# Prompt attention of a hybrid decoder layer in packs of up to eight key blocks, and merge gates stored raw

## Chip, core and metric

One Trainium2 chip, one of its cores. The metric is the device time of one execution in microseconds (us). The kernel before takes 1359.62 us, the median of 3 runs (1356.57 to 1366.08).

## What is computed

One layer of a decoder trunk, for a prompt of 1024 tokens and for 8 sequences of 4 new tokens with 512 tokens in a cache (32 more rows). The width D is 1024, all data is fp32. In short:

```python
h = rms_norm(x) * norm_g
(q, kv, gate, z_a, q_g, k_g, v_g, a_low, z_b, merge) = split(h @ w_in)
# NSA attention: 8 query heads in 2 groups of 4 (G = 2, R = 4), head width 64
o_cmp = softmax over compressed keys (one per 16 tokens)
o_slc = softmax over 16 selected blocks of 64 keys   # a prompt of 1024 has 16: all causal keys
o_win = softmax over a window of 512 keys
o_nsa = (g0 * o_cmp + g1 * o_slc + g2 * o_win) * silu(z_a)      # g0, g1, g2: sigmoid(gate)
o_g   = rms_norm(gated linear attention(q_g, k_g, v_g, a_low)) * gla_g * silu(z_b)
g_a, g_b = split(merge)
mix   = sigmoid(g_a) * (o_nsa @ w_branch_a) + sigmoid(g_b) * (o_g @ w_branch_b)
y     = rms_norm(x + mix @ w_out) * final_norm_g
```

Scores carry a bias linear in the distance (ALiBi), `-slope * distance`. The new key and value rows, the new window buffers and the states of the linear attention are outputs too.

## The kernel before

Activations and weights are split into a high and a low part (fp32r), and a projection is three products: high x high, low input x high weights, high input x low weights. The projections are done in **units**: one unit is a third of the 1056 rows for one weight tile, 8 x 3 products of 352 columns (L240), into one bank of PSUM. There are 132 units, 117 of them (NE) up to the last group of heads and 15 (NLATE) beside it. Their banks alternate, 3 and 2 (`unit_of`, L317), so that a unit needs the bank of the unit but one before it to be read (`unit_out`, L325). ScalarE takes a unit out of its bank (L360); for the kinds za, zb, ma and mb with a sigmoid (L359), for the others as a copy. For za and zb VectorE then multiplies the bank by it (L373, L375). With the last unit of a tile ScalarE rounds a coming weight tile to its high part (L219), VectorE subtracts the low part (L227). A unit leaves for HBM from one of five buffers, by a DMA of SP. Units 34 to 45 are of za, 46 to 69 of zb, 70 to 93 of ma, 94 to 116 of mb.

The **main attention** is the stage in question. A row of work n = (r, i, br) is a head r of each group, 128 queries i (0 to 7) and a branch br (0 selected, 1 window). It has i + 1 key blocks of 128 keys, at most 5 in the window: 64 rows and 264 blocks. The two groups g are computed beside each other, so each block is two score passes, two transposes and two value passes. Blocks are cut in order into steps of four: 66 steps. Per row, in this order:
- `scores` (L1633 to L1647): TensorE multiplies queries by keys, into bank g.
- `score` on VectorE (L1985 to L2004): adds the bias, writes the scores to sP in SBUF and keeps the row's extreme for the exponential.
- `probs` on ScalarE (L2236 to L2246): the exponential over a whole row, in place in sP, and its sum (128 instructions, a table load where the engine comes from a sigmoid).
- `transposes` (L1649 to L1663): TensorE turns the blocks of a step, into banks 4 and 5; ScalarE copies bank 4 to pPT (`pT_copy`, L2248, its instruction at L2199), VectorE bank 5 (L2012).
- `values` (L1665 to L1681): TensorE multiplies by the values, into a region of bank 6 or 7 for each row.
- After each four rows `spread` (L1683 to L1697): the weights `gate / sum` are formed on VectorE (`weigh`, L2018 to L2031), turned and spread over 64 rows by 16 products of `ident` by `wcol`, copied out by ScalarE (L2199), multiplied into the outputs by VectorE (`drain`, L2033 to L2038), and added to oTn by GpSimd (L1853 to L1860). There are 16 of these.

The order is written by hand in each engine's loop. On TensorE (L1793 to L1822) step m is: the units of that step, transposes(m), values(m-1), scores(m+3), and a spread where four rows have ended. On VectorE (L2175 to L2195): all units of the step but one, the scores of m+3, weigh, the copy, the last unit. On ScalarE (L2312 to L2325): the exponentials of all rows whose last block lies in step m+1 or before, all units but one, the copies, the last unit. `units_at` (L1116) deals 76 units to the 49 steps before M0 = 49. The 17 steps from M0 on are the **tail**: the rows with r = 3 that are left, with attention of the 32 decode rows between them by a list of slots (`tail_step`, and on TensorE the second half of the loop), and one late unit in each of 15.

Around it: before 382 us lie the first projections and the compressed branch; behind 1005 us the linear attention, then the **merge stage**, where the products with w_branch_a and w_branch_b are multiplied on VectorE by the merge gates, which come back from HBM (`staged`, L2765 and L2780).

## Time and profile before

| | |
|---|---|
| runs | 1356.57, 1359.62, 1366.08 us; median 1359.62 |
| profiled execution | span 1354.8 us (the profile gives no other time for it) |
| TensorE, products | 1298.8 us busy, 96% of the span, 9533 instructions |
| TensorE, weight loads | 1170.1 us, 86% |
| VectorE (DVE) | 619.4 us, 46%, 1387 instructions |
| ScalarE (ACT) | 621.8 us, 46%, 1072 instructions |
| GpSimd (POOL) | 145.7 us, 11%, 184 instructions |
| chain that ended last | TensorE 56%, of it L240 31% |

The table says how long each engine had at least one instruction under way in one execution. TensorE's products are pipelined: the time from one start to the next is shorter than an instruction's own time, so the cost of a product is read from the starts. Weight loads (PEld) overlap them. PEclk is the clock that TensorE was granted, as a share of full speed; DMA is the mean busy share of 16 DMA engines.

### The profile page before, as it was taken

To read this page: it belongs to the slowest core of one execution; us is meant where nothing else is said; L and a number is where in the kernel's file an instruction comes from. 1 tells how busy PE (TensorE), PEld (TensorE's weight loads), DVE (VectorE), ACT (ScalarE), POOL (GpSimd) and SP (SyncE) were. 2 spreads that over 40 slices of the span, in tenths; PEclk is the share of its full clock that TensorE was granted. 3 is DMA by queue.
4 is the path that set the end of the run, shared out by engine and by line. 5 is a ranking of instruction groups with operands and counts; after the bars stand their busy time and mean duration, and the time that the engine had idled before them with its cause. 6 is when DMAs were issued, how large, how long until landed. Compare 5 with 4: busy or idle time off the path is not lost.

```text
span 1354.8 us, 23612 instructions
## 1 busy us (share of the span) xinstructions
PE 1298.8 (96%) x9533; PEld 1170.1 (86%) x9533; DVE 619.4 (46%) x1387; ACT 621.8 (46%) x1072; POOL 145.7 (11%) x184
## 2 busy tenths in 40 slices
PE   5999998999999999999999999999988989999998
PEld 4999998999988889989888889888866779999876
DVE  6211145645834343433323333466578767453342
ACT  6211336542555536666556645665467542221121
POOL 2100001103300000000000300313010260000000
PEclk9999999999999999999999999999999999899999
DMA  7251453522422211122212221554345656452331
GB/s 207 63 171 42 120 149 103 147 69 61 79 69 59 64 59 60 48 79 64 65 59 79 60 59 52 172 168 147 101 155 197 245 180 193 136 157 64 109 121 59
DMA packets 156908, 145.27 MB, mean 107 GB/s; under 512 B 27360, under 2 KB 141360, under 8 KB 156736
## 3 DMA queue, kind: packets, MB, share of 16 engines
q1 hardware_dynamic: 154016, 135.33, 33.1%
q0 software_dynamic: 2784, 8.43, 2.1%
q8 instruction: 76, 1.25, 0.4%
q14 instruction: 32, 0.26, 0.1%
HBM read 105.88 MB, written 41.88 MB: 109 GB/s over the span
## 4 chain that ended last, share of the span: by engine, by line
PE 56%; ACT 2%; DVE 2%; issue 1%; SPq 0%; DMA 0%; another core or an unknown queue 0%; POOL 0%; DVEq 0%; ACTq 0%
PE ps L240 31%; PE ps L2536 7%; PE ps L1645 4%; PE ps L1679 4%; PE ps L1661 3%; PE ps L1694 1%; PE ps L2443 1%; PE ps L2411 1%; DVE S L2648 1%; PE ps L2447 1%; PE ps L1764 1%; PE ps L2544 1%; PE ps L2502 0%; DMA m_raw<-in_w_branch_a 0%; SPq L3012 0%
## 5 line engine op out<-in xcount | busy, mean ns | idle before, releaser
L240 PE MATMUL ps<-hH,wH 128*128 128x352 f32 (+1 forms) x1320 | 440.0, 333 | 5.8 <-DVE stg L375 3.0
L240 PE MATMUL ps<-hH,wL 128*128 128x352 f32 (+1 forms) x1320 | 425.3, 322 | 0.0
L240 PE MATMUL ps<-hL,wH 128*128 128x352 f32 (+1 forms) x1320 | 424.8, 322 | 0.0
L240 PEld LDWEIGHTS ps<-hH,wH 128*128 128x128 f32 (+1 forms) x1320 | 248.1, 188 | 32.9 <-issue 26.5
L240 PEld LDWEIGHTS ps<-hL,wH 128*128 128x128 f32 (+1 forms) x1320 | 249.1, 189 | 2.2 <-issue 1.9
L240 PEld LDWEIGHTS ps<-hH,wL 128*128 128x128 f32 (+1 forms) x1320 | 247.8, 188 | 0.3
L227 DVE TENSOR_TENSOR wL<-w_raw,wH 128x1024 fp32r<-128x1024 f32 (+1 forms) x70 | 87.8, 1254 | 132.8 <-ACT wH L219 132.7
L2002 DVE CUSTOM_DVE_ANT_0 sP<-ps,dist,stat 128x256 f32<-128x256 f32 (+3 forms) x116 | 58.6, 542 | 176.8 <-issue 108.2
L360 ACT ACTIVATE stg<-ps 128x352 f32<-128x352 f32 x132 | 61.1, 463 | 119.1 <-PE ps L240 117.3
L219 ACT ACTIVATE wH<-w_raw 128x1024 fp32r<-128x1024 f32 (+1 forms) x70 | 73.5, 1050 | 70.5 <-issue 39.5
L2199 ACT ACTIVATE pPT<-ps 128x512 f32<-128x512 f32 x74 | 44.1, 596 | 131.9 <-PE ps L1661 131.8
L2245 ACT ACTIVATE sP<-sP,stat 128x640 f32<-128x640 f32 (+7 forms) x128 | 93.0, 728 | 12.0 <-DVE stat L2002 10.4
L2002 DVE CUSTOM_DVE_ANT_0 sP<-ps,dist 128x128 f32<-128x128 f32 (+3 forms) x128 | 46.5, 408 | 88.9 <-PE ps L1645 88.9
L1645 PE MATMUL ps<-kT,qT 64*128 64x256 f32 (+3 forms) x440 | 74.9, 450 | 0.0
L1679 PE MATMUL ps<-pPT,vtok 128*64 128x128 f32 x1056 | 73.0, 279 | 1.1 <-issue 1.1
L1859 POOL TENSOR_TENSOR tmp<-tmp 128x256 f32<-128x256 f32 x16 | 16.5, 1032 | 491.0 <-DVE tmp L2037 491.0
L1661 PE MATMUL ps<-ident,sP 128*128 128x128 f32 x528 | 68.7, 273 | 0.1
L1679 PEld LDWEIGHTS ps<-pPT,vtok 128*64 128x64 f32 x1056 | 56.5, 136 | 12.8 <-issue 12.6
L240 PE MATMUL ps<-ogH,m_wH 128*128 128x352 f32 x192 | 62.9, 328 | 2.7 <-DVE ogL L2754 2.7
L240 PE MATMUL ps<-ogH,m_wL 128*128 128x352 f32 x192 | 63.4, 330 | 0.0
L240 PE MATMUL ps<-ogL,m_wH 128*128 128x352 f32 x192 | 63.2, 329 | 0.0
L1661 PEld LDWEIGHTS ps<-ident,sP 128*128 128x128 f32 x528 | 61.0, 140 | 2.3 <-issue 0.8
(391 smaller groups left out, 2035.1 us busy)
## 6 DMA issues: line engine op xcount, KB each, us to landing
w_raw<-in_w_in SPq DMA_DIRECT2D x61, 512.0 KB, 4.1
p_spill<-stg SPq DMA_DIRECT2D x132, 176.0 KB, 1.8
zt<-p_spill SPq DMA_DIRECT2D x24, 528.0 KB, 4.8
w_raw<-in_w_in SPq DMA_DIRECT2D x17, 256.0 KB, 3.8
gvT<-p_spill SPq DMA_DIRECT2D x8, 528.0 KB, 5.4
x_all<-in_x_prompt SPq DMA_DIRECT2D x8, 512.0 KB, 10.0
m_raw<-in_w_branch_b SPq DMA_DIRECT2D x8, 512.0 KB, 5.5
xr<-in_x_prompt SPq DMA_DIRECT2D x8, 512.0 KB, 3.5
```

The source lines that it names most:

```text
L219: nc.scalar.activation(self.wH[:, c % 2, 0:n], self.raw[:, c % self.nraw, 0:n], ACT.Copy)\
L227: nc.vector.tensor_tensor(self.wL[:, c % 2, 0:n], self.raw[:, c % self.nraw, 0:n], self.wH[:, c % 2, 0:n].bitcast(F32), ALU.subtract).then ...
L240: mm = nc.tensor.matmul(ps[0:t.m, bank, 0:NF], w[:, c % 2, t.m * k:t.m * k + t.m], x[n][:, k, :], start=(k == 0 and i == 0), stop=(k == t. ...
L360: nc.scalar.activation(stg[:, u % NSTG, :], ps[:, bank, 0:NF], func, scale=DK ** -0.5 if t.kind == "gq" else 1.0).then_inc(sem("f_act"), 1)
L1645: mm = nc.tensor.matmul(ps[:, g, P * f:P * (f + w)], qT[rows, r, P * i:P * i + P], kT[rows, br, P * k0:P * (k0 + w)], start=True, stop=True)
L1661: mm = nc.tensor.transpose(ps[:, 4 + g, P * (f + k):P * (f + k) + P], sP[:, g, P * b:P * b + P], ident[:, :])
L1679: mm = nc.tensor.matmul(ps[HD * g:HD * g + HD, 6 + j % 2, col:col + P], vtok[:, key, P * br + HD * g:P * br + HD * g + HD], pPT[:, m % NPT ...
L1859: link(nc.gpsimd.tensor_tensor(t[:, 0:2 * P], t[:, 0:2 * P], t[:, 2 * P:4 * P], ALU.add))
L2002: nc.vector.tensor_tensor_reduce(sP[:, g, P * (spot[n] + c):P * (spot[n] + c + w)], ps[:, g, P * f:P * (f + w)], dist[:, b0:b0 + P * w], s ...
L2199: copy = lambda dst, src: nc.scalar.activation(dst, src, ACT.Copy)
L2245: nc.scalar.activation(p, p, ACT.Exp, bias=mcol[:, 2 * (n % 8) + g:2 * (n % 8) + g + 1], scale=-1.0, accum_out=lcol[:, j % 2, g, br, i % 2 ...
L2536: mm = nc.tensor.matmul(ps[0:n, bank, :], m, w[half][:, k, :], start=(k == 0 and i == 0), stop=(k == KT - 1 and i == 2))
```

## The change

The attention is taken in **packs**. For each r of 0 to 2 a list PACKS names nine packs of one to three rows with at most eight blocks together: 27 packs, 54 steps, of which some are shorter than four blocks; a row may begin in the middle of a step. The row order follows the list. The rows of r = 3 stay as 17 tail steps. On TensorE a pack is: its units, both steps' transposes, the scores of the pack after the next in two steps, both steps' values. A pack has three units, packs 0, 5, 10, 15, ... two. Scores and transposes of a pack alternate over four banks (0 and 1, 4 and 5), so scores wait for the copies out of the transposes' banks. A row's scores that lie in two banks are read by one VectorE instruction. The bias of a whole window row has a tensor of its own, dist5.

The weights go on before the transposes: VectorE forms `max(sum, TINY)` and its reciprocal for a row (two small instructions) and multiplies the row's exponentials in sP by it and by the gate, one `tensor_scalar` with two per-query scalars for each group (`weigh`), a pack ahead of the transposes. With that the spreading products, their copies, the products in `drain` and GpSimd's adds go. The outputs of all rows of a half (four query blocks of 128) add up in one bank, 6 or 7, and one VectorE instruction for each half adds it to oTn: 8 of them.

In a pack ScalarE takes the exponentials of the next pack first, then all units but one, both copies, the last unit. VectorE: the scores of the next pack, a drain where a half has ended, all units but one, both copies, weighing of the next pack, the last unit.

The units of ma and mb are copied out without the sigmoid. ScalarE takes the sigmoid of a merge gate in the merge stage, in place over 1056 columns, 16 times (`merge_gate`), and VectorE's products wait for it. Waits of SP and of the linear attention that named the spreads name what takes their place. The core of the diff:

```diff
-                func = ACT.Sigmoid if t.kind in ("za", "zb", "ma", "mb") else ACT.Copy
+                func = ACT.Sigmoid if t.kind in ("za", "zb") else ACT.Copy
...
+        PACKS = [((3, 0), (3, 1)), ((4, 1), (2, 0)), ((5, 1), (2, 1)), ((6, 0), (0, 0)), ((5, 0), (1, 0)),
+                 ((6, 1), (1, 1), (0, 1)), ((7, 0),), ((4, 0),), ((7, 1),)]
+        NPK = len(PACKS)
+        NS0 = NPK * (R - 1)
+        M0 = 2 * NS0
+        U = [(r, i, br) for r in range(R - 1) for pack in PACKS for i, br in pack]
+        NU0 = len(U)
+        U += [(R - 1, i, br) for i in range(PT) for br in range(2)]
         blocks_of = [i + 1 if br == 0 else min(i + 1, 5) for r, i, br in U]
-        spot = [9, 0, 1, 22, 19, 16, 0, 4, 19, 14, 0, 19, 12, 0, 8, 0, 23, 5, 6, 8, 20, 0, 3, 7, 19, 0, 5, 19, 0, 7, 0, 19,
-                0, 1, 2, 4, 17, 21, 0, 4, 19, 0, 17, 5, 10, 19, 0, 19, 8, 0, 1, 9, 11, 21, 17, 0, 14, 6, 0, 19, 6, 0, 16, 0]
-        cuts, cut_of, fill = [[]], {}, 0
-        for n in range(len(U)):
+        spot, cuts, cut_of = [0] * NU0, [[] for m in range(M0)], {}
+        pack_rows, n = [], 0
+        for M in range(NS0):
+            f, rows = 0, PACKS[M % NPK]
+            pack_rows.append(range(n, n + len(rows)))
+            for x in rows:
+                spot[n] = 8 * (M % 3) + f
+                c = 0
+                while c < blocks_of[n]:
+                    w = min(blocks_of[n] - c, 4 - f % 4)
+                    cuts[2 * M + f // 4].append((n, c, w, f % 4))
+                    for k in range(w):
+                        cut_of[n, c + k] = 2 * M + f // 4
+                    f, c = f + w, c + w
+                n += 1
+        spot += [14, 1, 12, 6, 3, 21, 15, 9, 2, 13, 7, 19, 6, 16, 4, 17]
...
+        def score_bank(m, g):
+            return (0, 4)[g] + m % 2 if m < M0 + 2 else g
+        def turn_bank_of(m, g):
+            return (0, 4)[g] + m % 2 if m < M0 else 4 + g
...
+            return UA * (M + 1) // NS0 - UA * M // NS0
...
+        def merge_gate(act, kind, f):
+            staged(act, kind, f)
+            z = z_of(kind, f)
+            nc.scalar.activation(z[:, :], z[:, :], ACT.Sigmoid).then_inc(sem("merge_gate"), 1)
+        def merge_gated(eng, kind, f):
+            eng.wait_ge(sem("merge_gate"), (0 if kind == "ma" else KT) + f + 1)
...
             def scores(m):
-                if m == 0:
+                if m < 2:
                     pe.wait_ge(sem("cmp_scored"), PT)
+                    pe.wait_ge(sem("cmp_pT"), PT)
+                elif m < 4:
+                    pe.wait_ge(sem("scored"), 2 * parts_to[1])
+                elif m <= M0 + 2:
+                    for name in ("pT_act", "pT_dve"):
+                        pe.wait_ge(sem(name), m - 3 if m < M0 + 2 else M0)
                 else:
                     pe.wait_ge(sem("scored"), 2 * parts_to[m - 1])
...
             def transposes(m):
-                if m == 0:
-                    pe.wait_ge(sem("cmp_pT"), PT)
+                if m < M0:
+                    pe.wait_ge(sem("scored"), 2 * parts_to[m + 2])
+                elif m == M0:
+                    pe.wait_ge(sem("pT_dve"), M0)
                 for g in range(G):
-                    pe.wait_ge(sem("probs"), 2 * cuts[m][-1][0] + g + 1)
-                    if m >= 1:
+                    pe.wait_ge(sem("weighed"), 2 * cuts[m][-1][0] + g + 1)
+                    if m > M0:
...
+                    j = 2 * r + i // 4
+                    first = j not in opened
+                    if first:
+                        opened.append(j)
+                        if j >= 2:
+                            pe.wait_ge(sem("o_added"), j - 1)
                     for k in range(w):
                         key = first_key(n) + c + k
+                        last = bank_end(j) == m and (n, c, w, f) == [x for x in cuts[m] if U[x[0]][1] // 4 == i // 4][-1]
                         for g in range(G):
                             mm = nc.tensor.matmul(
-                                ps[HD * g:HD * g + HD, 6 + j % 2, col:col + P],
+                                ps[HD * g:HD * g + HD, 6 + j % 2, P * (i % 4):P * (i % 4) + P],
                                 vtok[:, key, P * br + HD * g:P * br + HD * g + HD],
                                 pPT[:, m % NPT, g, P * (f + k):P * (f + k) + P],
-                                start=c + k == 0, stop=c + k == blocks_of[n] - 1)
+                                start=first and k == 0, stop=last and k == w - 1)
                 mm.then_inc(sem("av_done"), 1)
-            def spread(j):
...
-            for m in range(LA):
-                if m >= 1:
-                    pe_units(pe)
-                scores(m)
-            for m in range(ncut):
+            scores(0)
+            scores(1)
+            pe_units(pe, 2)
+            scores(2)
+            scores(3)
+            for M in range(NS0):
+                pe_units(pe, units_at(M))
+                transposes(2 * M)
+                transposes(2 * M + 1)
+                scores(2 * M + 4)
+                if M < NS0 - 1:
+                    scores(2 * M + 5)
+                values(2 * M)
+                values(2 * M + 1)
+            for m in range(M0, ncut):
                 t = m - M0
-                pe_units(pe, units_at(m))
+                pe_units(pe, int(t < NLATE))
                 slot(t, 0)
                 transposes(m)
-                if m >= 1:
+                if t >= 1:
                     values(m - 1)
                 slot(t, 1)
                 if m + LA < ncut:
@@ -1814,12 +1861,9 @@
                     pe.wait_ge(sem("scored"), 2 * len(parts))
                     diagonals(0, 0)
                 slot(t, 3)
-                for j in closed(m - 1):
-                    spread(j)
             unit_out(pe, NU - 1)
             turn_tails(pe, 0, 0)
             values(ncut - 1)
-            spread(4 * R - 1)
...
             def copies(m):
                 dve.wait_ge(sem("pT_ready"), 2 * m + 2)
                 if m >= NPT:
                     dve.wait_ge(sem("av_done"), m - NPT + 1)
                 w = cuts[m][-1][2] + cuts[m][-1][3]
-                nc.vector.tensor_copy(pPT[:, m % NPT, 1, 0:P * w], ps[:, 5, 0:P * w]).then_inc(sem("pT_dve"), 1)
-                if m < M0:
...
+                nc.vector.tensor_copy(pPT[:, m % NPT, 1, 0:P * w], ps[:, turn_bank_of(m, 1), 0:P * w])\
+                    .then_inc(sem("pT_dve"), 1)
+            def weigh(n):
+                r, i, br = U[n]
+                w, row = lcol[:, 2 * (n % 8):2 * (n % 8) + 2], P * spot[n]
+                dve.wait_ge(sem("probs"), 2 * n + 2)
+                link(nc.vector.tensor_scalar(w, w, TINY, None, ALU.max))
+                link(nc.vector.reciprocal(w, w))
                 for g in range(G):
-                    l, w = lcol[:, j % 2, g, :, :], wcol[:, j % 2, g, :, :]
-                    link(nc.vector.tensor_scalar(w, l, TINY, None, ALU.max))
...
+                    p, c0 = sP[:, g, row:row + P * blocks_of[n]], 8 * (br + 1) + R * g + r
+                    nc.vector.tensor_scalar(p, p, w[:, g:g + 1], gate[:, i, c0:c0 + 1], ALU.mult, ALU.mult)\
+                        .then_inc(sem("weighed"), 1)
+            weighed = 0
+            def weigh_rows(first, last):
+                nonlocal weighed
+                while weighed < len(U) and cut_of[weighed, 0] <= first and last_cut(weighed) <= last:
+                    weigh(weighed)
+                    weighed += 1
             def drain(j):
-                dve.wait_ge(sem("w_copied"), j + 1)
-                dve.wait_ge(sem("av_done"), last_cut(4 * j + 3) + 1)
-                nc.vector.tensor_tensor(tmp[:, j % 2, :], tmp[:, j % 2, :], ps[:, 6 + j % 2, :], ALU.mult)\
-                    .then_inc(sem("O_out"), 1)
+                r, ip = divmod(j, 2)
+                o = oTn[:, r, 4 * P * ip:4 * P * ip + 4 * P]
+                dve.wait_ge(sem("av_done"), bank_end(j) + 1)
+                if j == 0:
+                    dve.wait_ge(sem("cmp_out"), PT)
+                nc.vector.tensor_tensor(o, ps[:, 6 + j % 2, :], o, ALU.add).then_inc(sem("o_added"), 1)
...
             def tail_step(m):
                 t = m - M0
+                weigh_rows(m, m + LA - 1)
                 slot(t, 0)
                 copies(m)
                 slot(t, 1)
                 if m + LA < ncut:
                     score(m + LA)
                 slot(t, 2)
-                for j in closed(m - 1):
+                for j in (closed(m - 1) if t else closed(M0 - 2) + closed(M0 - 1)):
                     drain(j)
-                for j in range(4 * R):
-                    if cut_of[4 * j + 3, 0] == m:
-                        weigh(j)
-                dve_units(dve, units_at(m))
+                dve_units(dve, int(t < NLATE))
+                weigh_rows(m + 1, m + LA - 1)
                 head_part(t)
             dve_units(dve)
-            for m in range(LA):
-                score(m)
...
+            score(0)
+            score(1)
+            dve_units(dve, 2)
+            weigh_rows(1, 1)
+            for M in range(NS0):
+                score(2 * M + 2)
+                score(2 * M + 3)
+                if M >= 1:
+                    for j in closed(2 * M - 2) + closed(2 * M - 1):
+                        drain(j)
+                dve_units(dve, units_at(M) - 1)
+                copies(2 * M)
+                copies(2 * M + 1)
+                weigh_rows(2 * M + 3, 2 * M + 3)
+                if M == 4:
                     link(nc.vector.memset(orow[:, :, :], 0.0))
                     decode_queries()
                     dve.wait_ge(sem("aup_high"), 1)
                     nc.vector.tensor_tensor(aupS[0:64, :], aupR[0:64, :], aupS[0:64, :].bitcast(F32), ALU.subtract)
-                for j in range(4 * R):
-                    if cut_of[4 * j + 3, 0] == m:
-                        weigh(j)
-                copies(m)
                 dve_units(dve)
-            drain(4 * R - 1)
+            score(M0 + 2)
+            for m in range(M0, ncut):
+                tail_step(m)
+            drain(2 * R - 1)
...
+            probs_to(-1, 1)
+            for M in range(NS0):
+                probs_to(-1, 2 * M + 3)
+                act_units(act, units_at(M) - 1)
+                pT_copy(2 * M)
+                pT_copy(2 * M + 1)
                 act_units(act)
+            for m in range(M0, ncut):
...
-                staged(dve, "ma", c)
+                merge_gated(dve, "ma", c)
...
                             mring.high(act, 1)
+                            merge_gate(act, "ma", 0)
...
+                if c >= 1:
+                    merge_gate(act, "ma", c)
                 mring.high(act, c + 2)
             for f in range(KT):
+                merge_gate(act, "mb", f)
...
```

## Rows read from the trace of the kernel before

**Rows 1.** Stages: from:to, length, each engine's busy us (count), PEclk, DMA share, GB/s.
```profile
382.00:858.00 476.00, 472.91 (x3581) 423.40 (x3582) 178.62 (x588) 270.90 (x453) 31.92 (x42) 1.00 0.21 65
858.00:1005.00 147.00, 139.57 (x1411) 115.79 (x1411) 89.75 (x259) 82.65 (x151) 23.48 (x31) 1.00 0.46 143
```

**Rows 2.** Timeline of TensorE, 502 to 507: start, us, line, operation, idle and releaser.
```profile
502.64 1.04 PE L1661 MATMUL ps<-ident,sP 128*128 128x128 f32 x8
503.61 1.09 PE L1679 MATMUL ps<-pPT,vtok 128*64 128x128 f32 x16
504.63 1.13 PE L1645 MATMUL ps<-kT,qT 64*128 64x512 f32 x4
505.69 1.09 PE L1694 MATMUL ps<-ident,wcol 128*64 128x128 f32 x16
506.72 0.43 PE L240 MATMUL ps<-hH,wH 128*128 128x352 f32 x1
506.98 0.32 PE L240 MATMUL ps<-hL,wH 128*128 128x352 f32 x1
507.14 0.32 PE L240 MATMUL ps<-hH,wL 128*128 128x352 f32 x1
```

**Rows 3.** Groups of lines: count, busy us, mean ns, idle before.
```profile
L1694 PE MATMUL ps<-ident,wcol 128*64 128x128 f32 x256 | 17.4, 278 | 0.0
```

**Rows 4.** Timeline of TensorE in the tail, 941 us.
```profile
941.06 0.60 PE L1764 MATMUL ps<-ident,kp 128*128 128x128 f32 x4
941.50 0.71 PE L1661 MATMUL ps<-ident,sP 128*128 128x128 f32 x5
```

**Rows 5.** Groups of lines on VectorE, each shape apart.
```profile
L227 DVE TENSOR_TENSOR wL<-w_raw,wH 128x1024 fp32r<-128x1024 f32 x69 | 87.0, 1261 | 128.9 <-ACT wH L219 128.8
L2012 DVE COPY pPT<-ps 128x512 f32<-128x512 f32 x66 | 45.4, 687 | 20.0 <-PE ps L1661 15.5 <-remote 2.3 <-issue 1.9
...
L375 DVE SCALAR_TENSOR_TENSOR stg<-ps,small,stg 128x352 f32<-128x352 f32 x24 | 13.8, 579 | 14.0 <-ACT stg L360 14.0
...
L302 DVE SCALAR_TENSOR_TENSOR bsumw<-w,small,bsumw 128x128 f32<-128x128 f32 x30 | 10.6, 352 | 1.1
...
L2026 DVE RECIPROCAL wcol<-wcol 128x4 f32<-128x4 f32 x32 | 5.7, 178 | 1.1
...
L300 DVE TENSOR_SCALAR bsumw<-w,small 128x128 f32<-128x128 f32 x2 | 0.6, 282 | 0.0
```

**Rows 6.** Timeline of VectorE in the tail, 988 to 991.
```profile
988.62 0.69 DVE L2062 CUSTOM_DVE_ANT_0 zS<-ps,zb 128x512 f32<-128x512 f32 x1 [1.28 <-PE ps L1718]
...
989.53 1.25 DVE L1371 SCALAR_TENSOR_TENSOR ls<-zl 128x1056 f32<-128x1056 f32 x1
990.70 0.68 DVE L1416 TENSOR_TENSOR Q1a<-qd,dec 128x512 f32<-128x512 f32 x1
```

**Rows 7.** Timeline of ScalarE, 507 to 513.
```profile
507.81 1.28 ACT L2245 ACT_TABLE_LOAD   x1
509.10 0.83 ACT L2245 ACTIVATE sP<-sP,stat 128x640 f32<-128x640 f32 x1
...
512.15 0.47 ACT L360 ACTIVATE stg<-ps 128x352 f32<-128x352 f32 x1
```

**Rows 8.** Groups of lines on ScalarE.
```profile
L2245 ACT ACTIVATE sP<-sP,stat 128x640 f32<-128x640 f32 (+7 forms) x128 | 93.0, 728 | 12.0 <-DVE stat L2002 10.4 <-issue 0.8
...
L2946 ACT ACTIVATE mixH<-zt 128x1056 fp32r<-128x1056 f32 x8 | 8.7, 1088 | 17.6 <-DVE zt L2784 17.6
```

**Rows 9.** Timeline of TensorE, 490 to 491.
```profile
490.32 0.66 PE L240 MATMUL ps<-hH,wH 128*128 128x352 f32 x1 [2.58 <-DVE stg L375]
490.79 0.49 PE L240 MATMUL ps<-hL,wH 128*128 128x352 f32 x1
491.08 0.49 PE L240 MATMUL ps<-hH,wL 128*128 128x352 f32 x1
```

**Rows 10.** Timeline of ScalarE in the linear attention, 1091 us.
```profile
1091.64 0.60 ACT L2878 ACTIVATE ogs<-ps 128x512 f32<-128x512 f32 x1 [1.68 <-PE ps L2478]
```

More of the change, by code:

```diff
@@ L1919, in _ @@
             reset_of(resets[1])
-            add(4 * R - 2)
             for n in range(NSTG):
@@ L2300, in tail_step @@
                     slot(t, place)
-                for j in closed(m - 1):
-                    spread(j)
                 if t == 2:
@@ L2312, in _, with probs_to @@
             rows = 0
-            for m in range(ncut):
-                while rows < len(U) and (last_cut(rows) <= m + LA - (1 if m >= M0 else 2) or cut_of[rows, 0] <= m):
+            def probs_to(first, last):
+                nonlocal rows
+                while rows < len(U) and (last_cut(rows) <= last or cut_of[rows, 0] <= first):
                     probs(rows)
                     rows += 1
-                if m >= M0:
-                    tail_step(m)
-                    continue
-                act_units(act, units_at(m) - 1)
-                copies(m)
+            probs_to(-1, 1)
[4 more added lines that the diff above has]
+                pT_copy(2 * M + 1)
                 act_units(act)
+            for m in range(M0, ncut):
+                probs_to(m, m + LA - 1)
+                tail_step(m)
             tail_keys(act, 0, 0)
             nc.scalar.activation(small[:, 159:160], zmin[0], ACT.Exp, scale=0.0)
-            spread(4 * R - 1)
         @block.sync
```

157 lines of the change are left out of this document (50 added, 107 removed).

## The prediction

> **What bounds the kernel now.** I read the stages first. From 382 to 858 us, the attention up to the last group of heads, TensorE works for 472.91 of 476.00 us at full clock, VectorE for 178.62 and ScalarE for 270.90 [rows 1]. The instructions of TensorE in order of time then show what fills it: one step of attention (8 transposes 0.97 us, 16 value passes 1.02, scores of four key blocks 1.06) between runs of projection products [rows 2]. Last come the groups of lines, for what VectorE and ScalarE must do in the shadow of TensorE. So only two things can move the time: TensorE instructions that go, and new waits of TensorE. The sum is made against the profiled execution, span 1354.8 us; the median of the runs, 1359.62, is 4.8 above it, and I put the difference found on the median.
>
> **Part 1, no spreading products.** A spread lasts from 505.69 to 506.72, 1.03 us [rows 2]. There are 256 passes in all, 16 to a spread, so 16 spreads [rows 3]; 11 of them belong to steps before 858 us. They lie in the dense stream of TensorE: -16.5 us. The copy on ScalarE, the product on VectorE and the adds on GpSimd that go with them were hidden and count nothing.
>
> **Part 2, packs.** Before 858 us there are 49 steps; there will be 27 packs. The 264 blocks with their transposes and value passes stay. What goes is the cost of changing from one kind of work to the next. Passes of one kind follow each other every 0.11 us (four in 0.44 [rows 4]). A step has 8 transposes, 8 pairs of value passes and the time of 8 pairs of score passes: 24 x 0.11 = 2.64 us. Measured are 0.97 + 1.02 + 1.06 = 3.05, and the first projection product behind them takes 0.26 where the next takes 0.16, so 3.15 [rows 2]: 0.51 per step, whatever its size. 22 fewer: -11.2 us. This needs the scores, which now write the banks that the transposes used, not to wait for the copies out of them. VectorE's copy, 0.69 [rows 5], can start 0.9 us after the start of the transposes, when the second group of the first cut is turned, and ends at 1.7; the second cut is turned at 1.86. Taken at nothing; if it misses, at most the 0.5 of a step in each of 27 packs, 13 us.
>
> **Part 3, the order on VectorE and ScalarE.** Before, ScalarE took exponentials of rows that were scored a step earlier. Now the exponentials of the next pack stand ahead of the unit copies of this pack, and a third unit needs the bank of the first. I follow a pack with 4 + 4 blocks and three units, from the start of the transposes before it. Their second copy ends at 1.86 + 0.1 + 0.69 = 2.6. VectorE then weighs the pack. A wide product of a row by two columns is not in the trace. The nearest are L300, 128 wide with one column, 0.28, and L302, the same with a second tensor, 0.35; L302 and L375 (352 wide, 0.58) give 1.0 ns per element, so L300 is cheaper by 0.07, the time of half its elements [rows 5]. From that I take 0.5 ns per element: 0.28 + 0.19 = 0.47 for 512, with 0.67 at the whole pace as the upper bound and 0.28, no more than the 128 wide one, as the lower. Operations overlap by about 0.08 (L1371 lasts 1.25, the next starts 1.17 after it [rows 6]). Two rows: four small ones of 0.2 (L2026 [rows 5]) and 4 x 0.39 are 2.4 us (3.2 at the upper bound), so 5.0. The product of the last gated unit, 0.5: 5.5; where that unit ends a weight tile L227 comes too, 1.2: 6.7. Scores of the first row, 2 x 0.61 (0.69 for 512 [rows 6], less the overlap), and 0.1 of signalling: 6.8 or 8.0. ScalarE: table 1.28, four exponentials at 0.73 [rows 7, 8]: 11.1 or 12.3. Table 1.28 and copy 0.47 of the first unit: 12.9 or 14.1. Its product on VectorE with signalling, 0.7: 13.6 or 14.8. TensorE wants the bank after three times 1.86 of attention, 0.1, and two units of 24 products at 0.16: 13.4. A wait of 0.2 or 1.4 us.
>
> This holds while the units are gated ones of za and zb, up to pack 10 (counted from 0). Rows of 6 or 7 blocks, or three rows, add 0.5 to 0.7. Packs 1 to 4 have the weight tile in the chain: 1.5, 2.1, 1.9, 2.1. Packs 6 to 8 meet short packs or one row of 8: nothing. Pack 9: 1.1. Packs 0, 5 and 10 have two units; there the copies of the turned probabilities come late, behind the sigmoid: 2.3, 3.8 (the decode queries stand in that chain) and 1.1. Together 16 us. The mechanism is seen once in the trace: TensorE waits 2.58 us for L375, and the products behind it start 0.29 us apart instead of 0.16, which is TensorE at the lower of its two levels, 1.2 GHz [rows 9]. That place goes, 2.6 and some 1.7 for the clock: -4.3. For the longest two or three new waits I put +3 for the clock. Sum: +14.7. Bounds: -4.3 without any wait, +24 with 0.9 more in ten packs.
>
> The raw merge units, packs 11 to 26, have neither table load nor product: the chain ends at 10 to 11.5 where TensorE wants 13.4. Nothing. Were that cover gone, 16 packs at 1 to 2 us would cost some 25.
>
> A rule speaks against the change here. First the rows: the exponential starts 0.01 us after its table load ends [rows 7], so a switch of tables costs 1.28. The Trainium skill (ScalarE: Activation LUTs, "What ACT_TABLE_LOAD costs") counts a drain of 1380 ns with every load, about 2.66 us for each switch. By the page the chain of a gated pack would be some 2.8 us longer. The trace disagrees with it.
>
> **Part 4, the tail** (858 to 1005 us). VectorE works 89.75 of 147 us [rows 1]. 66 blocks are weighed: 32 products, 15 us, and 32 small ones, 6, less the old weights and drains, 7: +14, into 57 us of idle time. It shows where a row is weighed just ahead of its transposes. The row of 8 blocks: scoring 0.7, table 1.3, exponentials 2.7, small ones 0.4, its first product 0.7, together 5.8; TensorE has a unit, 3.9, and some decode work meanwhile: a wait of 0 to 1.9, I take 1.2. The last row, 5 blocks, is weighed behind L2062 and L2064, which end at 989.6, while the transposes stand right behind the scores that L2062 reads from 988.6 [rows 6]: small ones 0.4, product 0.5, and the second group's: +2.1. L1371 and the state inputs start 1.35 later too. Some 0.8 of this falls into waits that are there anyway. +2.5, bounds 0 and +8.
>
> **Part 5, sigmoids in the merge stage.** 16 more of 1.09 us [rows 8] on an engine with room. The first, with its table 2.4 us, stands ahead of L2878, before which ScalarE idles 1.68 [rows 10] and for which TensorE waits: +0.7; a second switch behind it, +0.3. +1, bounds 0 and +5.
>
> **Sum:** -16.5 - 11.2 + 14.7 + 2.5 + 1 = -9.5: a span of 1345, a median of 1350. This kernel's measurement can tell about 1%, 13.6 us, from no change: 1346.0 and 1373.2.
>
> **The rivals.**
> A, as summed: 1350, own range 1342 to 1357. Chance 0.41.
> B, the chain is shorter than I make it and TensorE never waits: -27.7 - 4.3 + 2 = -30, so 1330, and up to 1340 with a few waits left. For it: every wait is 1 to 2 us at the end of ten terms. 0.25.
> C, weighing at 1.0 ns per element: +8 in the gated packs, +4.5 in the tail: 1362. Against it stands the 0.07 between L300 and L302. 0.12. The Trainium skill (VectorE: DVE Perf Modes, "The perf-mode tier table") lists this kind of operation in fp32 out of SBUF at two elements a cycle, against C; L300 agrees.
> D, the change doesn't save what packs promise: scores wait for the copies in all of them, 13 us: 1363. Against it, 0.1 to 0.2 us of room. 0.09.
> E, slower: VectorE's chain is as in C, and after every wait TensorE runs slow. Place: the third unit of the gated packs, the tail. Price: 12.5, and 1.7 [rows 9] in nine places, 15: 1378. It decides once new waits pass 46 us, of which A has 22. For it, VectorE is late in one chain everywhere; against it, after its one wait the clock fell only once. 0.11.
> F, a switch of tables costs twice its load, 2.6 more in ten packs: 1376. Against it [rows 7]. 0.02. The page's drain is of that size.
>
> Faster by over 1%: B and the lower part of A, 0.36. Slower by over 1%: E and F but for their mild ends, 0.11. Within: 0.53. The range 1332 to 1366 leaves out the ends of B, E and F.
>
> **What would show it.** Right: no products of ident by wcol; between two runs of projection products one block of transposes, scores and values of 5.6 us; products of sP 512 wide at 0.47 (C: 0.67); a wait on the VectorE product of za or zb ahead of the third unit of packs 1 to 4 (B: none), and of scores on the copies in packs 0 and 5 (D: in all); no table loads in the second half of this stage; the low clock at one to three places (E: nine); a wait of the last transposes of the tail for VectorE; the exponential right behind its table load (F: not). Wrong would make it waits in the raw packs, or a tail longer by over 8 us.

## The result, and the profile after

The changed kernel takes 1355.23 us (median of 14 runs, 1351.3 to 1357.64), the kernel before 1361.43 us (14 runs): a ratio of 0.995, 95% interval 0.9936 to 0.9965. That is 6.2 us less; forecast were 9.6 less, down to 1350. Of the 5.2 us between 1350 and 1355.23, 1.8 are the kernel before, whose median was 1359.62 when the forecast was made. The profiled execution has a span of 1349.9 us, 4.9 less than before's.

The stages first, as in [rows 1], but cut where the tail begins and where the first state product stands:

```profile
382.20:852.60 470.40, 454.50 (x3402) 416.25 (x3402) 217.04 (x555) 193.29 (x393) 16.12 (x20) 1.00 0.22 66
852.60:999.00 146.40, 137.04 (x1294) 110.96 (x1294) 98.06 (x259) 78.20 (x145) 18.17 (x25) 0.97 0.46 144
```

Before, the same landmarks are 476.1 and 147.8 us apart. The stage gained 5.8 us, the tail 1.4; everything behind the tail lost 2.0, and what lies ahead of the stage 0.4. TensorE works 18.4 us less in the first stretch, but the stretch is only 5.8 shorter: it now stands idle in between. The view of waits says for whom (columns: who waited and for whom, us in total, times, longest):

```profile
PE ps L1690 <- DVE pPT L2045: 11.2, 9, 4.0
PE ps L240 <- DVE stg L375: 4.7, 4, 2.0
...
PE ps L1382 <- ACT zl L1484: 2.2, 2, 1.5
PE ps L1706 <- DVE sP L2057: 2.1, 1, 2.1
```

L1690 are the scores, which wait for the copies out of the banks that they share with the transposes; L240 a third unit that waits for its bank. A pack in the quiet part of the stage, TensorE in order of time, answers [rows 2]:

```profile
711.31 1.91 PE L1706 MATMUL ps<-ident,sP 128*128 128x128 f32 x16
713.23 2.01 PE L1690 MATMUL ps<-kT,qT 64*128 64x512 f32 x12
715.17 1.97 PE L1729 MATMUL ps<-pPT,vtok 128*64 128x128 f32 x32
717.07 0.43 PE L240 MATMUL ps<-hH,wH 128*128 128x352 f32 x1
717.33 0.32 PE L240 MATMUL ps<-hL,wH 128*128 128x352 f32 x1
```

5.76 us for eight blocks, where two steps of before take 2 x 3.05 = 6.10; and one slow entry to the projection products instead of two. No spreads. VectorE's weighing, each width by itself, answers [rows 5]:

```profile
L2057 DVE TENSOR_SCALAR sP<-sP,stat,gate 128x640 f32<-128x640 f32 x40 | 22.9, 615 | 0.7
...
L2057 DVE TENSOR_SCALAR sP<-sP,stat,gate 128x1024 f32<-128x1024 f32 x8 | 6.1, 809 | 0.1
...
L2057 DVE TENSOR_SCALAR sP<-sP,stat,gate 128x128 f32<-128x128 f32 x16 | 4.8, 358 | 0.3
```

From 128 to 1024 elements 451 ns, 0.50 ns each, on top of 0.29: 0.54 for 512. The slope is the forecast one, the fixed part was taken 0.07 too low.

The chain that was forecast for gated packs can be read off one of them, VectorE and then ScalarE, up to the unit that TensorE waits for:

```profile
441.50 0.69 DVE L2045 COPY pPT<-ps 128x512 f32<-128x512 f32 x1 [0.18 <-PE ps L1706]
442.11 0.16 DVE L2053 TENSOR_SCALAR stat<-stat 128x2 f32<-128x2 f32 x1
...
444.22 0.60 DVE L2057 TENSOR_SCALAR sP<-sP,stat,gate 128x128 f32<-128x128 f32 x2
444.74 0.58 DVE L375 SCALAR_TENSOR_TENSOR stg<-ps,small,stg 128x352 f32<-128x352 f32 x1
445.24 1.21 DVE L227 TENSOR_TENSOR wL<-w_raw,wH 128x1024 fp32r<-128x1024 f32 x1
446.37 0.95 DVE L2036 CUSTOM_DVE_ANT_0 sP<-ps,dist 128x768 f32<-128x768 f32 x1
...
454.32 1.08 DVE L375 SCALAR_TENSOR_TENSOR stg<-ps,small,stg 128x352 f32<-128x352 f32 x2 [5.43 <-ACT stg L360]
```
```profile
448.28 1.28 ACT L2283 ACT_TABLE_LOAD   x1 [5.32 <-DVE stat L2036]
449.57 0.94 ACT L2283 ACTIVATE sP<-sP,stat 128x768 f32<-128x768 f32 x1
...
452.53 1.28 ACT L360 ACT_TABLE_LOAD   x1
453.82 0.82 ACT L360 ACTIVATE stg<-ps 128x352 f32<-128x352 f32 x2
```
```profile
454.96 0.43 PE L240 MATMUL ps<-hH,wH 128*128 128x352 f32 x1 [1.66 <-DVE stg L375]
```

The transposes began at 439.56. The second copy ends 2.6 us later, weighing at 5.3, the low part of the weight tile at 6.9, the first row's scores at 8.6, the exponentials at 12.9, and TensorE goes on at 15.4.

**The clock.** The last thing to see is PEclk by stretches of 5 us. In the kernel before it is under 1 behind the stage's start in two places, at 490 (behind the wait of [rows 9], which is gone now) and at 1155 to 1165; the sum of (1 - clock) x 5 us is 5.1. In the changed kernel there are six places, here the first three:

```profile
495.00:500.00 5.00, 2.10 (x8) 1.16 (x8) 3.36 (x7) 2.86 (x5) 0.00 (x0) 0.75 0.10 36
500.00:505.00 5.00, 5.00 (x51) 4.60 (x50) 2.87 (x7) 2.74 (x4) 0.00 (x0) 0.90 0.12 39
855.00:860.00 5.00, 3.46 (x10) 1.42 (x10) 0.84 (x2) 2.90 (x5) 0.10 (x1) 0.59 0.78 258
860.00:865.00 5.00, 5.00 (x25) 5.00 (x24) 4.02 (x10) 2.08 (x5) 0.00 (x0) 0.72 0.19 39
980.00:985.00 5.00, 3.27 (x24) 2.71 (x24) 4.86 (x12) 1.44 (x3) 0.00 (x0) 0.72 0.62 218
```

and at 985, 1060 to 1070, 1100 to 1110 and 1150 to 1160: the sum is 13.8. This is not one execution's luck. Each run has a mean granted clock, and (1 - clock) x span is the time that the low level costs if TensorE had work in all of it, an upper bound. Means of the runs in us; "the rest" is the time less that bound:

| kernel | runs | time | clock | low clock | the rest |
|---|---|---|---|---|---|
| before | 23 | 1361.2 | 0.9913 | 11.9 | 1349.3 |
| changed | 14 | 1354.7 | 0.9861 | 18.8 | 1335.8 |
| e1_no_spreads | 6 | 1347.5 | 0.9898 | 13.7 | 1333.8 |
| e2_merge_only | 12 | 1362.7 | 0.9893 | 14.6 | 1348.1 |
| e3_merge_undone | 12 | 1359.4 | 0.9867 | 18.0 | 1341.4 |
| e4_weigh_later | 5 | 1333.9 | 0.9918 | 10.9 | 1323.0 |
| e5_weigh_twice | 5 | 1389.3 | 0.9768 | 32.2 | 1357.1 |
| e6_one_then_four | 5 | 1333.9 | 0.9916 | 11.2 | 1322.7 |
| e7_last_row_early | 5 | 1332.3 | 0.9920 | 10.7 | 1321.7 |
| e8_twice_later | 6 | 1347.7 | 0.9890 | 14.8 | 1332.9 |
| e9_steps_of_four | 6 | 1371.5 | 0.9847 | 21.0 | 1350.5 |
| e10_later_merge_undone | 6 | 1335.5 | 0.9910 | 12.0 | 1323.5 |
| e11_unit_first | 6 | 1346.1 | 0.9887 | 15.2 | 1330.8 |

In two more groups of 11 runs the kernel before has 11.2 and 10.1 for the low clock and the same rest, 1349.1 and 1349.5. How much of the bound is time can be read within one kernel: over the 45 runs of before, a run with 1 us more of it took 0.76 us more (a straight line through the runs, standard error 0.04), and over the 14 of the changed kernel 0.75 (0.14). So without the clock the change gives 13.5 us if the bound counts in full, or 11.8 if three quarters of it do, and 6.9 or 5.2 of them go back to the clock.

### The profile page after: what moved, and what is told of

The parts are those of the page before. It is cut to its first block, busy times and chain, and to the rows that moved or that the text cites. A ratio compares the mean times of both kernels' runs of the same rounds, so it can differ in the third digit from the quotient of the medians.

```text
span 1349.9 us, 22855 instructions
## 1 busy us (share of the span) xinstructions
PE 1280.1 (95%) x9229; PEld 1159.8 (86%) x9229; DVE 666.8 (49%) x1352; ACT 559.2 (41%) x1025; POOL 120.7 (9%) x154
## 4 chain that ended last, share of the span: by engine, by line
PE 62%; DVE 7%; ACT 5%; issue 2%; DVEq 0%; another core or an unknown queue 0%; ACTq 0%
PE ps L240 36%; PE ps L2567 7%; PE ps L1690 4%; PE ps L1729 4%; PE ps L1706 4%; ACT sP L2283 1%; DVE sP L2057 1%; DVE sP L2036 1%; PE ps L2474 1%; PE ps L2442 1%; DVE pPT L2045 1%; PE ps L2575 1%; PE ps L1637 1%; PE ps L2533 1%; ACT gjunk L2883 1%
## 5 line engine op out<-in xcount | busy, mean ns | idle before, releaser
L240 PE MATMUL ps<-hH,wH 128*128 128x352 f32 (+1 forms) x1320 | 437.8, 332 | 7.5 <-DVE stg L375 4.7
L240 PE MATMUL ps<-hH,wL 128*128 128x352 f32 (+1 forms) x1320 | 425.9, 323 | 0.0
L240 PE MATMUL ps<-hL,wH 128*128 128x352 f32 (+1 forms) x1320 | 425.1, 322 | 0.0
L240 PEld LDWEIGHTS ps<-hH,wH 128*128 128x128 f32 (+1 forms) x1320 | 248.2, 188 | 21.3 <-issue 13.6
L240 PEld LDWEIGHTS ps<-hL,wH 128*128 128x128 f32 (+1 forms) x1320 | 249.4, 189 | 2.2 <-issue 1.9
L240 PEld LDWEIGHTS ps<-hH,wL 128*128 128x128 f32 (+1 forms) x1320 | 248.0, 188 | 0.3
L360 ACT ACTIVATE stg<-ps 128x352 f32<-128x352 f32 x132 | 60.7, 461 | 147.8 <-PE ps L240 147.0
L2045 DVE COPY pPT<-ps 128x512 f32<-128x512 f32 (+1 forms) x71 | 45.5, 651 | 140.5 <-PE ps L1706 140.0
L2238 ACT ACTIVATE pPT<-ps 128x512 f32<-128x512 f32 (+1 forms) x79 | 44.4, 569 | 94.6 <-PE ps L1706 94.6
L2036 DVE CUSTOM_DVE_ANT_0 sP<-ps,dist 128x640 f32<-128x640 f32 (+7 forms) x128 | 77.6, 658 | 9.9 <-PE ps L1690 9.9
L1690 PE MATMUL ps<-kT,qT 64*128 64x512 f32 (+3 forms) x392 | 70.9, 484 | 11.2 <-DVE pPT L2045 11.2
L1729 PEld LDWEIGHTS ps<-pPT,vtok 128*64 128x64 f32 x1056 | 57.7, 138 | 12.9 <-issue 11.1
L1729 PE MATMUL ps<-pPT,vtok 128*64 128x128 f32 x1056 | 68.5, 280 | 0.0
L2057 DVE TENSOR_SCALAR sP<-sP,stat,gate 128x640 f32<-128x640 f32 (+7 forms) x128 | 65.4, 555 | 2.3
L240 PE MATMUL ps<-ogH,m_wH 128*128 128x352 f32 x192 | 62.3, 324 | 2.7 <-DVE ogL L2785 2.7
L240 PE MATMUL ps<-ogH,m_wL 128*128 128x352 f32 x192 | 63.0, 328 | 0.0
L240 PE MATMUL ps<-ogL,m_wH 128*128 128x352 f32 x192 | 62.8, 327 | 0.0
```

Of the source, the lines that this page charges most:

```text
L240: mm = nc.tensor.matmul(ps[0:t.m, bank, 0:NF], w[:, c % 2, t.m * k:t.m * k + t.m], x[n][:, k, :], start=(k == 0 and i == 0), stop=(k == t. ...
L360: nc.scalar.activation(stg[:, u % NSTG, :], ps[:, bank, 0:NF], func, scale=DK ** -0.5 if t.kind == "gq" else 1.0).then_inc(sem("f_act"), 1)
L1690: mm = nc.tensor.matmul(ps[:, score_bank(m, g), P * f:P * (f + w)], qT[rows, r, P * i:P * i + P], kT[rows, br, P * k0:P * (k0 + w)], start ...
L1729: mm = nc.tensor.matmul(ps[HD * g:HD * g + HD, 6 + j % 2, P * (i % 4):P * (i % 4) + P], vtok[:, key, P * br + HD * g:P * br + HD * g + HD] ...
L2036: nc.vector.tensor_tensor_reduce(sP[:, g, P * (spot[n] + c):P * (spot[n] + c + w)], found, bias, slope_of(r, g), 3e38 if c == 0 else low, ...
L2045: nc.vector.tensor_copy(pPT[:, m % NPT, 1, 0:P * w], ps[:, turn_bank_of(m, 1), 0:P * w])\
```

## The experiments

All ratios are to the kernel before, with 95% intervals. "The stage" is from the first scores of the main attention to the tail, in the profiled execution.

**e1_no_spreads**: the first part of the change alone. The outputs are left unweighted, so the result is not that of the layer.

```diff
             def spread(j):        # TensorE
-                for br in range(2):
...
-                mm.then_inc(sem("w_spread"), 1)
+                pe.sem_inc(sem("w_spread"), 1)
             def spread(j):        # ScalarE
-                copy(tmp[:, j % 2, :], ps[:, 4, :]).then_inc(sem("w_copied"), 1)
+                act.sem_inc(sem("w_copied"), 1)
```

> The kernel before, with the spreads left out: TensorE's 16 x 16 products of ident by wcol and ScalarE's copies of them are gone, and drain copies the outputs instead of multiplying them, so rows are not weighted. All else stands, steps of four blocks too. If the stream of TensorE is what sets the time and nothing hides behind the spreads (my theory): -16.4 us, 16 times 1.03, ratio 0.988, no new waits. Rival 1: the spreads give the copies of the turned probabilities their time; without them TensorE waits at transposes or values instead, and the gain is under 8 us, 0.995. Rival 2: the clock: if it falls in fewer places, 2 to 4 us more, 0.985.

Measured: 0.9891 (0.9870 to 0.9912), 14.8 us less. The stage went from 476.1 to 466.1, with one new wait of 0.57. With the low clock counted in full it is 15.5. The term holds within the interval: TensorE's own work in its stream counts nearly in full.

**e2_merge_only** and **e3_merge_undone**: the merge part added to before, and taken out of the changed kernel.

```diff
-                func = ACT.Sigmoid if t.kind in ("za", "zb", "ma", "mb") else ACT.Copy
+                func = ACT.Sigmoid if t.kind in ("za", "zb") else ACT.Copy
...
+                if c >= 1:
+                    merge_gate(act, "ma", c)
```

> The kernel before with only the merge part of the change: ma and mb stored raw, 16 sigmoids over 1056 columns in the merge stage. Theory: the main stage had no waits that table loads caused, so it gains nothing there; the stage behind 1005 us pays 1 us, as forecast, or up to 3.5 with another fall of the clock: ratio 1.000 to 1.003. Rival: the raw units free ScalarE so far that the one wait of before, 2.58 us at 490, or others go: 0.997. Rival: the sigmoids delay TensorE in the merge stage: +5 or more, 1.004.

> The changed kernel with the merge part undone: units of ma and mb (packs 11 to 26) are taken out with a sigmoid again, no sigmoids in the merge stage. Theory, by my chain: the first unit's bank comes free at 12.4 to 13.2 us after the transposes, TensorE wants it at 13.4, so packs of three units hardly wait; packs 15, 20 and 25, of two units, wait 1 to 3 us each for late copies. +4 to +7 in this stage, -1 to -3 behind it: ratio to before 0.996 to 0.999 (the changed kernel has 0.995). Rival: every one of the 16 packs waits 1 us or more: +16 and more with the clock, 1.005 to 1.010. Rival: nothing waits: 0.993 to 0.995.

Measured: e2 1.0011 (0.9998 to 1.0024), some 1.5 us more and not clear of nothing; e3 0.9984 (0.9967 to 1.0001), 4.6 us more than the changed kernel. In e3's trace the packs of raw units, now with sigmoids again, wait for a unit's bank in four places, 0.92 us at 751 us and three times 0.27 or 0.28; what else it costs stands at the tail's first step, where a wait of 1.54 us (L1382 of the changed kernel) becomes 4.30. So table loads beside the packs were affordable, as the chain said, and raw gates are worth a little only with packs. In the stretch that is the same code in both kernels, packs 0 to 5, the clock fell in three places (455, 475 and 500 us) in e3 and in one in the changed kernel, on waits that are alike within 0.1 us: the length of a wait alone does not decide whether it falls.

**e4_weigh_later**: does VectorE's order set the waits?

```diff
             for M in range(NS0):
                 score(2 * M + 2)
                 score(2 * M + 3)
+                weigh_rows(2 * M + 1, 2 * M + 1)
...
                 copies(2 * M + 1)
-                weigh_rows(2 * M + 3, 2 * M + 3)
```

> The changed kernel, but VectorE weighs a pack's rows behind the scores of the pack after it instead of ahead of them (two to three us of VectorE's work leave the chain: copies, weighing, scores, exponentials, unit copy, TensorE). Theory: each wait of packs 0 to 5 and 9 gets shorter by 2.4 us or goes: of 2.22, 0.62, 1.66, 2.03, 3.98 and 0.35 only some 1.5 is left in pack 5, and the clock no longer falls at 497 us: -9.3 and -1.75, ratio to before 0.987. The short packs' 0.65 stay. Rival: the waits come from ScalarE's order alone (exponentials ahead of the units) with VectorE off the chain: they stay, 0.995. Rival: weighing late comes too late for the transposes: new waits on sP, over 0.997.

Measured: 0.979 (0.9769 to 0.9812), more than expected. The stage takes 456.8 instead of 470.4 us, and the view of waits has no L375 in it any more:

```profile
383.80:840.70 456.90, 452.25 (x3402) 415.49 (x3402) 220.40 (x552) 197.31 (x400) 16.62 (x20) 1.00 0.23 68
840.70:984.20 143.50, 135.64 (x1294) 110.59 (x1293) 98.44 (x260) 76.11 (x137) 18.41 (x26) 0.96 0.46 145
```
```profile
PE ps L1690 <- DVE pPT L2045: 4.6, 7, 0.9
...
PE ps L1706 <- DVE sP L2057: 2.7, 2, 2.1
```

Pack 0's wait of 2.22 is gone and pack 5's 3.98 is 0.48: the chain behind both kinds of wait was the same. With the low clock counted in full it is 12.8 us less than the changed kernel, near the waits that went from the stage, 15.9 to 4.6 us; the clock gives another 7.9 (6.0 at three quarters), where I had counted one fall of 1.75. That is the larger part of the surprise; the waits gave 11.3 where I had 9.3. It is a version that beats both kernels.

**e5_weigh_twice** and **e8_twice_later**: the same extra work, ahead of the scores and behind them.

```diff
                 for g in range(G):
+                    link(nc.vector.tensor_scalar(p, p, 1.0, None, ALU.mult))
                     nc.vector.tensor_scalar(p, p, w[:, g:g + 1], gate[:, i, c0:c0 + 1], ALU.mult, ALU.mult)
```

> The changed kernel with a second product over each row (by 1.0) ahead of the weighing: VectorE's cost of weighing doubled, some 0.5 us for each of two products of a row, 2 us for a pack of two rows. Theory: weighing stands in the chain that ends with the first unit's bank, so each wait of packs 0 to 5 and 9 grows by 2 us, packs 6 to 8 and 10 get one of up to 1: +15, the raw packs behind (chain 10 to 11.5, TensorE wants the bank at 13.4) stay without one, the tail +2, the clock +1 to +4: ratio 1.007 to 1.012 (changed kernel: 0.995). Rival: weighing is beside the chain: only the tail grows, 0.997. Rival: VectorE becomes the bound in the raw packs too: 16 more waits, over 1.02.

> e4_weigh_later with the second product by 1.0 of e5_weigh_twice: the same added work on VectorE, 128 products, but behind the scores. In e5 it gave 14 us of new waits and 13 of lower clock and took the ratio from 0.995 to 1.021. Theory: here nothing waits for it between 382 and 841 us; only the tail pays, as in e5, 5 to 10 us: from 0.979 to between 0.983 and 0.987. Rival: what cost so much in e5 is VectorE's load or its traffic in SBUF, not the place in the chain: over 0.995.

Measured: e5 1.0214 (1.0187 to 1.0242), e8 0.9918 (0.9892 to 0.9945), both above their ranges. The stage, e5 and then e8:

```profile
383.50:880.60 497.10, 467.85 (x3401) 427.19 (x3401) 258.49 (x651) 192.24 (x392) 16.10 (x21) 0.97 0.21 62
```
```profile
382.40:839.20 456.80, 452.16 (x3401) 415.44 (x3401) 261.45 (x647) 197.24 (x400) 16.98 (x20) 1.00 0.22 68
```

VectorE does 41 us more than without the second product in both (217.04 and 220.40 before). Ahead of the scores the stage grows by 26.7 us; behind them by nothing, 456.8 to 456.8. In e5 the waits for L375 are 13.5 us instead of 4.7 and those for the copies 15.2 instead of 11.2; pack 10's grows from 0.88 to 2.73, and one raw pack of sixteen waits, 0.55. All new waits of the stage are 13.4 us, near the 15 expected. The clock was not: 32.2 instead of 18.8, that is 13.4 more (10 at three quarters) where I had put 1 to 4. The total alone, over 1.02, would have pointed at the second rival; the one raw pack that waits speaks against it. Both explanations that compete with the place in the chain, VectorE's load and its traffic, are out for the stage. The tail pays more than I expected in e8, 156.5 instead of 143.6 us: there transposes wait for weighed rows in 13 places:

```profile
PE ps L1706 <- DVE sP L2058: 11.2, 13, 2.7
```

**e11_unit_first**: the same waits, taken away on ScalarE.

```diff
+                early = int(M < 11 and units_at(M) == 3)
+                act_units(act, early)
                 probs_to(-1, 2 * M + 3)
-                act_units(act, units_at(M) - 1)
+                act_units(act, units_at(M) - 1 - early)
```

> The changed kernel, but in packs 1 to 4 and 6 to 9 ScalarE takes the first unit out before the exponentials of the next pack; VectorE's order stands. The same waits, taken away on the other engine. Theory: the waits for L375 in packs 1 to 4 and 9, 4.7 us, go; packs 0 and 5 (two units) keep theirs, 6.2; in packs where the exponentials then end late, the copies of the turned probabilities come up to 1 us late: ratio 0.991 to 0.994 against 0.995. Rival: those late copies cost as much as the waits that go: 0.995 to 0.998.

Measured: 0.9895 (0.9863 to 0.9926), a bit under my range. The four waits for L375 are gone, those of packs 0 and 5 stand (2.21 and 3.98), and no copy came late: the rival is out. In packs of three units the wait needed two things, VectorE's order and ScalarE's; either of them changed removes it.

**e6_one_then_four** and **e7_last_row_early**: what is left in e4.

```diff
+            f = 3 if sum(i + 1 if br == 0 else min(i + 1, 5) for i, br in rows) == 5 else 0
...
-                weigh_rows(m, m + LA - 1)
+                weigh_rows(m + 1 if t == 14 else m, m + LA - 1)
```

> e4_weigh_later (weighing behind the scores, 0.979), and packs of five blocks are turned as one block and then four instead of four and then one. Theory: in these packs the scores behind the transposes wait 0.66 us for VectorE's copy of a first step of four blocks (0.69, from 0.97 on, while the transposes end at 1.25); with one block first, its copy ends at 0.9 and nobody waits: six waits of 0.66 go, -4, ratio 0.976. Rival: the copy of the second step, now of four blocks, is waited for by the second scores or the values instead: 0.979.

> e6_one_then_four, and the last row of the tail is weighed at the start of its step, in VectorE's idle time before the copy, not behind the decode scores. Theory: TensorE's wait of 2.13 us for the weighed row goes, and what stands behind it on VectorE (the inputs of the linear attention) comes 1.5 us earlier: -2 to -3.5, with one fall of the clock less perhaps another -1.7: ratio 0.972 to 0.974. Rival: TensorE then waits for something else of the same step: 0.976.

Measured: e6 0.9809 (0.9780 to 0.9838), e7 0.9802 (0.9774 to 0.9829); both above their forecasts (0.976, and 0.972 to 0.974), and neither can be told from e4. The first is a miss: the waits of 0.66 us went, five of them, but scores into a bank of one block are over so early that those behind them wait for the second copy, in five other packs:

```profile
503.79 0.49 PE L1691 MATMUL ps<-kT,qT 64*128 64x128 f32 x4
504.66 1.13 PE L1691 MATMUL ps<-kT,qT 64*128 64x512 f32 x4 [0.38 <-DVE pPT L2046]
```

The stage stays at 456.7, as the rival had it. In e7 the tail's wait of 2.14 us is gone and one of 1.08 stands behind it: tail 144.1 to 139.1 us, most of it a fall of the clock that this execution lacks; in the means it is 1.6.

**e9_steps_of_four**: the packs of e4 cut into two steps again.

```diff
-                pe_units(pe, units_at(M))
+                pe_units(pe, units_at(M) - 1)
                 transposes(2 * M)
...
+                pe_units(pe)
                 transposes(2 * M + 1)
```

> e4_weigh_later with each pack split again into two steps on every engine: TensorE does its units but one, one step's transposes, values and scores, the last unit, the other step's. So 27 more groups of attention work between projection products, all else the same. Theory: a change of kind costs 0.51 a group as forecast; the changed kernel's packs measure 5.75 for what two steps of before do in 6.10, and 0.1 less at the projection product: 0.45: +12 to +14, ratio 0.988 to 0.989. Rival: the saving is not in the changes of kind, it costs nothing or less than 4 us: 0.979 to 0.982. Rival: new waits of scores for copies: over 0.992.

Measured: 1.009 (1.0065 to 1.0114), the last rival: scores wait for copies, up to 3.11 us. As a price of the change of kind the total is useless: the copies of a step now stand behind a unit on ScalarE and VectorE, and the stage has 17.3 us of waits against 4.6 and three falls of the clock (5.1 us). A step without waits does tell it:

```profile
526.82 1.04 PE L1706 MATMUL ps<-ident,sP 128*128 128x128 f32 x8
527.78 1.09 PE L1729 MATMUL ps<-pPT,vtok 128*64 128x128 f32 x16
528.81 1.13 PE L1690 MATMUL ps<-kT,qT 64*128 64x512 f32 x4
529.87 0.43 PE L240 MATMUL ps<-hH,wH 128*128 128x352 f32 x1
```

3.05 us, to the hundredth the step of before. And 30.8 us more in the stage, less 12.7 of waits and 5.1 of clock, are 13.0 for 27 more groups: 0.48 each, or 0.52 if the falls count at three quarters.

**e10_later_merge_undone**: e7 without the merge part, an edit as in e3.

> e7_last_row_early (weighing behind the scores, 0.980) with the merge part undone: sigmoids of ma and mb back in the units. In the changed kernel undoing it cost 4.6 us (e3). Theory: those came from the same chain, and with 2.4 us less in it the table loads of packs 11 to 26 are covered: nothing in this stage, -1 behind it: 0.979 to 0.981. Rival: the loads delay something else (copies of packs of two units, the tail's first step, 4.30 us in e3): 0.983 to 0.985.

Measured: 0.9823 (0.9794 to 0.9852); stage 457.2 against 456.7, and in the packs of ma and mb no wait for a unit, only those for copies that e6 has too. With the shorter chain the table loads cost at most 0.5 us there. Between my case and the rival's the total doesn't decide; the tail's first wait, 2.08 against 0.95, is the rest of what e3 showed.

## Why the prediction was right, and where not

The direction, the terms and the place of the waits were right; the time came out 5.2 us above the forecast median and inside its own range, with 3.4 us less gained than forecast.

**Part 1**, -16.5: the spreads took 11.3 us of the stage and 5.1 of the tail in before's trace, 16.3, and e1 measured 14.8, with 16.4 inside its interval. Right.

**Part 2**, -11.2: 22 fewer groups at 0.34 a pair in the attention (6.10 to 5.76) and 0.1 at the projection product are 9.7; e9's difference gives 0.48 a group, 10.6. The stage's balance agrees. Ahead of the tail the changed kernel has also done two blocks more of transposes and scores and six more of values (396 transposes against 392, 792 value passes against 768), at the forecast's pace of 0.11 some 2.2 us. So -5.8 is -11.3 for spreads, +12.9 for waits (15.9 against 3.0), +2.2, and -9.6 for 22 groups; one fall of the clock stands in either stage. Right within 0.6 to 1.6 us. The condition, that scores don't wait for copies, held in packs of eight with three units as worked out: 16 transposes in 1.91 us and no idle time behind them. It was not worked out for packs of five blocks, where the transposes are over at 1.25 us and the first copy at 1.9: six waits of 0.66 to 0.85 us, 4 us that the sum didn't have. That is rival D in small.

**Part 3**, +16 of waits: 15.9 in the trace, partly by luck. Packs 0, 5 and 10: forecast 2.3, 3.8 and 1.1, found 2.22, 3.98 and 0.88. Packs 1 to 4: 1.5, 2.1, 1.9, 2.1 against 0, 0.62, 1.66, 2.03; pack 9 1.1 against 0.35. The 4.0 us that were too much there make up for the 4 of the short packs; that the sum came out is luck. That VectorE's weighing stands in this chain was the core of the forecast; e4, e5 and e8 show it with the work unchanged, doubled, and doubled elsewhere. The raw packs' cover held too (e5: one wait in sixteen packs).

**The table loads.** The exponential starts 0.01 us after its load, as at 449.57 above, and so does the unit's copy, 1.29 behind the start of its own (452.53 to 453.82); in the changed kernel's trace 38 of 42 loads are followed like this, and the other four by an instruction that waits for VectorE. Rival F is out. The Trainium skill (ScalarE: Activation LUTs, "What ACT_TABLE_LOAD costs") counts a drain of 1380 ns with every load, by an estimate from it 2.8 us more in this chain; the traces disagree with it. On the weighing it was right: the Trainium skill (VectorE: DVE Perf Modes, "The perf-mode tier table") has this product at two elements a cycle, and 0.50 ns per element agree with it.

**Part 4**, +2.5 in the tail: idle time of TensorE went from 7.4 to 9.4 us, of it 2.14 for the last row, forecast 2.1. Not in the sum was the last addition of outputs (L2076), for which the linear attention's transposes (L1400) wait; the view of that line lists who waited for it:

```profile
PE ps L1400: 1.8, 1
```

In the kernel before they waited 0.5 us there, for the last drain (1004.88). In return two waits of 1.08 and 1.11 us are gone. **Part 5**, +1: e2 has 1.5, between -0.3 and 3.3, which agrees but can't be told from nothing.

**The step that was mis-sized is the clock**: "For the longest two or three new waits I put +3 for the clock", less 1.7 for the old wait, +1.3 net. Measured are +8.7 in the profiled executions (13.8 against 5.1) and +6.9 in the means (18.8 against 11.9), upper bounds both; at three quarters they are 6.6 and 5.2. Two things were wrong in it. I took one execution of before as its state: by its mean clock, 0.995, the low level cost it 6.8 us, where the mean of 23 runs is 11.9. And I charged the longest waits alone, with sure falls at one to three places, where there are six; the runs show that a wait of the same length brings one in one execution and not in another, and that one of 1.54 us in the tail did it too. Without the clock my sum was -10.8 and the runs give between -11.8 and -13.5; the 1.0 to 2.7 between them I can't assign to a part.

## What to carry over

When work is added to an engine with room, ask behind what it stands, not how busy the engine is: in the stage, 41 us of VectorE's work cost 26.7 us ahead of the scores, half of it waits and the rest lower clock, and nothing behind them. Where a dense TensorE stream is the bound, price a wait at its length and then again for the clock: here 11.3 us of waits less gave 6 to 7.9 more through it. And take the clock from the mean of many runs, since one profile shows one draw.

## What the runs showed of the hardware

The mean granted clock takes few values from run to run of the same kernel: of 45 runs of before, 5 had 0.997 (1353.7 to 1355.7 us), 15 had 0.993 (1358.0 to 1361.1) and 18 had 0.989 (1361.8 to 1365.0); the other seven had values close to these. A step is some 4 us. At a wait of 3.98 us and at one of 1.54 it fell to the lower level (1.2 GHz) and in the same execution not at 2.22, 1.66 and 2.03. While it is low the transposes take twice as long (eight in 1.90 us for the last row of e4, 965.12 to 967.02, and 0.97 elsewhere). The Trainium skill (TensorE: Matmul & The Clock Gate, "Part 1: The HAM clock gate (the "warmup" mystery)") says that the gate follows how busy TensorE has recently been and that its effect differs from run to run of one kernel; these runs agree. An all-fp32 product of a tensor in SBUF by two per-partition columns takes 0.29 us and 0.50 ns per element, 128 to 1024 wide.
